# Sums of the resident operand made ahead and parked in DRAM, and result tiles added to the rows in DRAM by accumulating DMAs

## The reference, cut to what matters

```python
def reference(x, mem, ...):                     # x (1, 2048, 1024) fp32, D_FF = 4096
        h = _rmsnorm(x, norm_mix_g[layer])
        proj = h @ w_in[layer]
        ...                                     # window attention, pooling, memory attention
        merged = (gates[:, :, 0] * (y_attn @ w_branch_attn[layer])
                  + gates[:, :, 1] * (y_pool @ w_branch_pool[layer])
                  + gates[:, :, 2] * (y_mem @ w_branch_mem[layer]))
        x = x + merged @ w_out[layer]
        hm = _rmsnorm(x, norm_mlp_g[layer])
        x = x + jnp.square(jax.nn.relu(hm @ w_up[layer])) @ w_down[layer]
    return _rmsnorm(x, norm_final_g)
```

## Time and profile before

| what | value |
|---|---|
| median of 3 runs | 3003.94 us (2999.12 to 3004.13) |
| the profiled execution: time, span | 3000.8 us, 2999.1 us |
| busy: PE, DVE, ACT, POOL | 2736.9, 1779.3, 994.4, 968.1 us |
| granted TensorE clock over the span | 0.959 |
| first part (to 1317 us) | 1317 us |
| second part, first matmul to last | 1333.5 to 2983.4 us |

### The profile page before, as it was taken

One profiled execution on the slowest core, in us unless ns is written; L12 is line 12 of the kernel. 1 busy time (PEld: TensorE's weight loads), 2 busy tenths in 40 slices (PEclk: granted clock), 3 DMA queues, 4 the chain that ended last, 5 costly groups with the idle time before them and its releaser, 6 DMA issues.

```text
span 2999.1 us, 33978 instructions
## 1 busy us (share of the span) xinstructions
PE 2736.9 (91%) x12449; PEld 2245.0 (75%) x12449; DVE 1779.3 (59%) x2098; ACT 994.4 (33%) x1714; POOL 968.1 (32%) x621
## 2 busy tenths in 40 slices
PE   8999999999999999967878999799988969789697
PEld 7788778887888778856767888688877758667586
DVE  4643355244633363357677666866676686775987
ACT  4543244324433353333233222322232232321342
POOL 0101110020001010134453332333345666665765
PEclk9999999999999999988988999899999989989899
DMA  5124322332233323343553334333343534535343
GB/s 183 53 85 133 113 64 81 120 124 81 67 121 104 95 70 112 106 147 112 168 169 116 110 111 137 107 109 111 110 158 136 186 131 137 183 133 172 138 146 134
DMA packets 276351, 365.48 MB, mean 122 GB/s; under 512 B 10024, under 2 KB 219996, under 8 KB 276188
## 3 DMA queue, kind: packets, MB, share of 16 engines
q1 hardware_dynamic: 273884, 355.01, 36.3%
q0 software_dynamic: 2304, 8.39, 0.8%
HBM read 271.09 MB, written 92.27 MB: 121 GB/s over the span
## 4 chain that ended last, share of the span: by engine, by line
PE 62%; issue 13%; POOL 10%; DVE 9%; DMA 5%; ACT 1%; SPq 0%; POOLq 0%; DVEq 0%; ACTq 0%
PE ps L1404 19%; PE ps L1405 19%; PE ps L1406 19%; POOL rows_tm L1366 5%; PE ps L1409 2%; DMA piece_f<-mrg_d 2%; DMA piece_f<-up_d 2%; DVE s_lo L1098 2%; DVE res_lo L1107 1%; POOL s_sum L1342 1%; POOL s_sum L1337 1%; PE ps L1554 1%; DVE rows_tm L1184 1%; PE ps L1537 1%; POOL piece_f L1339 1%
## 5 line engine op out<-in xcount | busy, mean ns | idle before, releaser
L1404 PE MATMUL ps<-res_hi,s_hi 128*128 128x512 f32 x2016 | 810.7, 402 | 179.7 <-issue 121.4
L1405 PE MATMUL ps<-res_lo,s_hi 128*128 128x512 f32 x2016 | 802.0, 398 | 0.0
L1406 PE MATMUL ps<-res_hi,s_lo 128*128 128x512 f32 x2016 | 800.6, 397 | 0.0
L1404 PEld LDWEIGHTS ps<-res_hi,s_hi 128*128 128x128 f32 x2016 | 390.5, 194 | 278.1 <-issue 152.6
L876 DVE TENSOR_TENSOR w_lo<-stage,w_hi 128x2048 fp32r<-128x2048 f32 (+1 forms) x125 | 234.9, 1879 | 459.1 <-ACT w_hi L589 459.1
L1404 PE MATMUL ps<-h_hi,w_hi 128*128 128x512 f32 x1216 | 485.0, 399 | 11.6 <-issue 11.6
L1406 PE MATMUL ps<-h_hi,w_lo 128*128 128x512 f32 x1216 | 476.6, 392 | 0.0
L1405 PE MATMUL ps<-h_lo,w_hi 128*128 128x512 f32 x1216 | 476.3, 392 | 0.0
L1098 DVE TENSOR_TENSOR s_lo<-piece_f,s_hi 128x512 fp32r<-128x512 f32 x288 | 283.9, 986 | 289.8 <-ACT s_hi L589 289.8
L1406 PEld LDWEIGHTS ps<-res_hi,s_lo 128*128 128x128 f32 x2016 | 388.9, 193 | 83.1
L1405 PEld LDWEIGHTS ps<-res_lo,s_hi 128*128 128x128 f32 x2016 | 390.3, 194 | 80.2
(11 more groups left out here) (170 smaller groups left out, 3332.2 us busy)
## 6 DMA issues: line engine op xcount, KB each, us to landing
stage<-in_w_gate SPq DMA_DIRECT2D x96, 512.0 KB, 4.5
rows_d<-rows_tm SPq DMA_DIRECT2D x32, 1024.0 KB, 5.1
piece_f<-in_w_up SPq DMA_DIRECT2D x32, 1024.0 KB, 6.2
up_d<-c SPq DMA_DIRECT2D x128, 256.0 KB, 2.4
piece_f<-up_d SPq DMA_DIRECT2D x32, 1024.0 KB, 7.6
rows_tm<-rows_d SPq DMA_DIRECT2D x32, 1024.0 KB, 5.5
stage<-in_w_in SPq DMA_DIRECT2D x60, 512.0 KB, 4.7
src<-in_w_down SPq DMA_DIRECT2D x12, 1024.0 KB, 11.3
```

Source lines behind the costliest of these rows:

```text
L1404: mm(dst, wh, xh, start=first, stop=False)
L1405: mm(dst, wh, xl, start=False, stop=False)
L1406: return mm(dst, wl, xh, start=False, stop=last)
```

## The change

**Resident sums.** They are no longer made at the turns. For the jobs whose resident is a weight (0, 3, 4, 5, 6) GpSimd makes them in the first part, at the start of each of the 4 blocks: for each job it loads two 128 x 1024 tiles (512 KB each) into a new buffer `tin`, makes four sums of 128x512 in place and stores the two tiles to a DRAM tensor `t_d`; five times in a row, each after the last one's stores have landed. For jobs 1 and 2 it does the same inside units 5 and 6 (two tile pairs each) and 10, 12, 14 and 16 (one pair each), as `ht_d` gets ready (`up_load`, `up_sums`). At a turn SP now loads all seven operands ready made (`load_slot`): slots 0 and 1 into `src` some units ahead, slots 2 to 6 straight into `res_raw`, each once the last unit's product of the same number is done.

**Rows.** Only jobs 0 and 6 still have rows in SBUF, and there DVE does the additions (`add_row`). In jobs 3, 4 and 5 (24 units) GpSimd issues four DMAs of 256 KB per unit that add the tile to the rows in DRAM (`add_in_place`); the loads and stores of `rows_tm` in these jobs are gone. A tile may be written anew when its DMA of the unit before has landed (`c_free`).

**Further.** `piece_f` has two buffers and SP loads piece n + 2 in unit n. Relu and square go from one DVE instruction to two of ACT. ACT scales the rows to be transposed, each half with a signal of its own. The factor of the norm is folded into the gain. The moving sums are made in the order S1, S3, S2, S4, and the order of the splits at a turn is changed.

```diff
+JOBS = 7
+W_JOBS = [0, 3, 4, 5, 6]
+
+UP_SUMS = {5: (1, (0, 1)), 6: (1, (2, 3)), 10: (2, (0,)), 12: (2, (1,)), 14: (2, (2,)), 16: (2, (3,))}
...
-    return 0 <= n < N_OUT or FIRST[3] <= n < NQT
+    return 0 <= n < N_OUT or FIRST[6] <= n < NQT
+
+
+def adds_apart(n):
+
+    return FIRST[3] <= n < FIRST[6]
...
+                if s < 2:
+                    sp.dma_start(src[:, s], slot_of(j, s)).then_inc(src_ld[s], 16)
+                    return
+                if j:
+                    sp.wait_ge(prod, PROD * (FIRST[j] - 1) + s + 1)
+                sp.dma_start(res_raw[:, s], slot_of(j, s)).then_inc(raw_ld[s - 2], 16)
...
-                sp.dma_start(piece_f[:], piece_of(n)).then_inc(pc_ld, 16)
+                sp.dma_start(piece_f[:, n % 2], piece_of(n)).then_inc(pc_ld[n % 2], 16)
...
+                    load_piece(n + 2)
+                if n in (N_OUT - 1, FIRST[2] - 3) or starts(n + 3) and n + 3 >= FIRST[3]:
+
+                    sp.wait_ge(r_lo_done, PROD * (j + 1))
+                    if j < 2:
+                        sp.wait_ge(up_t_st[0], 64 if j == 0 else 192)
+                        sp.wait_ge(up_t_st[1], 64)
+                        for r in range(2):
+                            sp.wait_ge(ht_st[r], 16 * 4 * (j + 1))
+                    for s in range(2):
+                        load_slot(j + 1, s)
...
-                    load_b21(job_of(n + 1))
+                            sp.wait_ge(add_st[s], 16 * (n - FIRST[3]))
+                    load_rows(n + 1)
+                if last:
+                    load_slot(j + 1, 2)
+                store_up(n, 0, c22, 1, 1)
+                if last:
+                    load_slot(j + 1, 3)
+                    load_slot(j + 1, 4)
+                store_up(n, 1, c11, 0, 0)
...
+            def relu_sq(n, which, order):
+
+                if not squares(n):
+                    return
+                tile, done = c_tile(n, which), 4 * up_quartets(n) + order
+                act.wait_ge(ev_dve, 7 * n + which)
+                op(tile[:], tile[:], ACT.Relu).then_inc(relu, 1)
+                act.wait_ge(relu, done)
+                op(tile[:], tile[:], ACT.Square).then_inc(u_rdy, 1)
...
+            def norm_tiles(n):
+
+                if not 0 <= n < N_OUT:
+                    return
+                act.wait_ge(rs_pow, n + 1)
+                act.wait_ge(row_st[row_slot(n)], 16 * (slot_uses(n) + 1))
+                for i in range(2):
+                    t = rows_of(n)[:, i, :]
+                    op(t, t, ACT.Copy, scale=rrs[:, i:i + 1]).then_inc(xn_done, 1)
...
-            def t1(j):
-
-                for i in range(2):
-                    dve.wait_ge(src_ld[i], 16 * (j + 1))
-                if j:
-                    dve.wait_ge(prod, PROD * (FIRST[j] - 1) + S1 + 1)
-                v.tensor_tensor(res_raw[:, 2], src[:, 1], src[:, 0], ALU.subtract).then_inc(t_done, 1)
...
-            def t2(j):
-
-                dve.wait_ge(src_ld[2], 16 * (j + 1))
-                dve.wait_ge(r_lo_done, PROD * j + 1)
-                dve.wait_ge(t_done, 2 * j + 1)
-                v.tensor_tensor(src[:, 0], src[:, 2], res_raw[:, 2], ALU.subtract).then_inc(t_done, 1)
+                dve.wait_ge(r_hi_done, PROD * j + s + 1)
+                v.tensor_tensor(res_lo[:, s], r_src(s), res_hi[:, s].bitcast(F32), ALU.subtract).then_inc(r_lo_done, 1)
+
+            def c_free(n, s):
+
+                if N_OUT < n <= FIRST[3]:
+                    dve.wait_ge(up_st[s], 16 * up_quartets(n))
+                elif FIRST[3] < n <= FIRST[6]:
+                    dve.wait_ge(add_st[s], 16 * (n - FIRST[3]))
...
+            def add_row(n, which, i, cols):
+
+                if not adds_rows(n):
                     return
-                tile = c_tile(n, which)
                 dve.wait_ge(ev_dve, 7 * n + which)
-                v.scalar_tensor_tensor(out=tile[:], in0=tile[:], scalar=0.0, in1=tile[:], op0=ALU.max, op1=ALU.mult)\
-                    .then_inc(u_rdy, 1)
+                dve.wait_ge(row_in[row_slot(n)], 16 * (slot_uses(n) + 1))
+                dst = rows_of(n)[:, i, cols * TB:(cols + 1) * TB]
+                v.tensor_tensor(dst, dst, c_tile(n, which)[:], ALU.add).then_inc(row_add, 1)
...
             for n in range(NQT):
-                j, first, last = job_of(n), starts(n), starts(n + 1) and n + 1 < NQT
+                j, first, last = job_of(n), starts(n), turns(n)
                 if first:
                     r_low(j, 3)
                 s_low(n, 6)
                 take_u2(n)
                 if last:
                     r_low(j + 1, 0)
-                    t1(j + 1)
-                if n == FIRST[6] - 1:
+                if n == FIRST[6] - 2:
                     dve.wait_ge(gf_ld, 16)
                     v.tensor_scalar(g_fin[:], g_fin[:], float(D) ** 0.5, None, ALU.mult).then_inc(gf_rdy, 1)
...
+                if first:
+                    r_low(j, 4)
                 s_low(n + 1, 0)
-                if has_norm(n - 1):
-                    scale_tile(n - 1)
+                if first:
+                    r_low(j, 5)
+                if last:
+                    r_low(j + 1, 1)
+                if is_final(n - 1):
+                    final_tiles(n - 1)
+                take_c22(n)
                 if first:
                     r_low(j, 6)
-                    r_low(j, 4)
-                    r_low(j, 5)
...
+                if last:
+                    r_low(j + 1, 2)
+                take(n, C21, A22, u3, 2)
+                add_row(n, C21, 1, 0)
...
+            def resident_sums(t, done, loaded):
+
+                b11, b12, b21, b22 = t[:, 0, 0:TB], t[:, 0, TB:D], t[:, 1, 0:TB], t[:, 1, TB:D]
+                pool.wait_ge(*loaded)
+                g_.tensor_tensor(b11, b12, b11, ALU.subtract).then_inc(t_sum, 1)
+                g_.tensor_tensor(b12, b22, b12, ALU.subtract).then_inc(t_sum, 1)
+                pool.wait_ge(t_sum, done * 4 + 1)
+                g_.tensor_tensor(b22, b22, b11, ALU.subtract).then_inc(t_sum, 1)
+                pool.wait_ge(t_sum, done * 4 + 3)
+                g_.tensor_tensor(b21, b21, b22, ALU.subtract).then_inc(t_sum, 1)
...
+                k1 = pool.snap(b + 4)
+                for i, j in enumerate(W_JOBS):
+                    k0 = 0 if j == 0 else KT * (j - 3)
+                    whole = w_outv if j == 0 else w_downv
+                    done = b * len(W_JOBS) + i
+                    if i:
+                        pool.wait_ge(t_st, done * 32)
+                        g_.tensor_tensor(flag[:, 3 + i:4 + i], m_half[:, 0:1], m_half[:, 0:1], ALU.add)
+                    for half, kb in enumerate((b, k1)):
+                        pool.dma_start(tin[:, 0, half, :], whole[:, bass.ds(kb + k0, 1), :].rearrange("p k n -> p (k n)"))\
+                            .then_inc(t_ld, 16)
+                    resident_sums(tin[:, 0], done, (t_ld, done * 32 + 32))
+                    pool.wait_ge(t_sum, done * 4 + 4)
+                    g_.tensor_tensor(flag[:, 8 + i:9 + i], m_half[:, 0:1], m_half[:, 0:1], ALU.add)
+                    for half, kb in enumerate((b, k1)):
+                        pool.dma_start(t_v[j][:, bass.ds(kb, 1), :].rearrange("p k n -> p (k n)"), tin[:, 0, half, :])\
+                            .then_inc(t_st, 16)
...
+            def up_load(j, ks):
+
+                if ks[0]:
+                    for i in range(len(ks)):
+                        pool.wait_ge(up_t_st[i], 32 * (uses(j, ks[i]) - 1))
+                for r in range(2):
+                    pool.wait_ge(ht_st[r], 16 * 4 * j)
+                pool.wait_ge(r_lo_done, PROD * j)
+                for i, k in enumerate(ks):
+                    for half in range(2):
+                        pool.dma_start(tin2[:, i, half, :], whole_of(j)[:, 4 * half + k, :]).then_inc(up_ld[i], 16)
+
+            def up_sums(j, ks):
+
+                for i, k in enumerate(ks):
+                    resident_sums(tin2[:, i], unit(j, k), (up_ld[i], 32 * uses(j, k)))
+                    pool.wait_ge(t_sum, 4 * unit(j, k) + 4)
+                    for half in range(2):
+                        pool.dma_start(t_v[j][:, 4 * half + k, :], tin2[:, i, half, :]).then_inc(up_t_st[i], 16)
+
+            def add_in_place(n, which, s, i, cols):
+
+                if not adds_apart(n):
+                    return
+                if n == FIRST[3]:
+
+                    for r in range(2):
+                        pool.wait_ge(row_st[r], 16 * (N_OUT // 2))
+                pool.wait_ge(ev_dve, 7 * n + which)
+                q = (n - FIRST[3]) % N_DOWN
+                pool.dma_start(rows_v[q][:, i, cols * TB:(cols + 1) * TB], c_tile(n, which)[:], accum_op=ALU.add)\
+                    .then_inc(add_st[s], 16)
...
             for n in range(NQT):
-                j, first, last = job_of(n), starts(n), starts(n + 1) and n + 1 < NQT
-                add_tile(n - 1, C12, 0, 1)
-                if first:
-                    t4(j)
+                if n in UP_SUMS:
```

(19 more changed lines are left out.)

301 lines of the change are left out of this document (129 added, 172 removed).

## The result

The changed kernel takes 2811.18 us (median of 4 runs, 2809.92 to 2819.84), the kernel before on the same chip 3002.78: a ratio of 0.937, 95% interval 0.9349 to 0.9391. The profiled execution of the changed kernel took 2819.84 us (span 2818.2), that of before 3000.8. It is the longest of the four, 8.7 us above the median, so what the two profiles show is 181 us of the 192 that the medians give.

The account below looks back on a forecast made before the run. It took TensorE's 19.04 us a unit as the floor, and the chain of sums, split and low part as the bound at turns. Terms -16 - 16 - 6 - 32 - 81 - 24 - 4 + 5 = -174 took 3000.8 to 2826 us, range 2785 to 2890.

Parts of the forecast that it names:

- Start of the second part: First part: GpSimd's added rounds of loads, sums and stores slow DVE now and then; +5 us, between 0 and 25.
- Rival (2): First part: GpSimd's rounds take 22 us, window sums come late and TensorE waits; +45 us, 2871 us; chance 0.08.
- Unit 0: Start of the second part: with slots loaded ready made, unit 0 takes 32 us for 47.9; -16 us.
- Units 1 to 5: Job 0: the wait for the scaled rows before the transposes goes, the ht wait stays; -16 us.
- Units 6 to 8: Job 1's sums, late slots and the norm's order still cost time: 28 + 35 + 30 = 93 for 99.2; -6 us.
- Turns 24 and 40: Up stores delay the slots, leaving small stalls: 27.5 us a turn for 44.0 and 43.0; -32 us.
- Turns 48, 56 and 64: No stores between the slots: 22.5 us for 49.5 and 50.3, 23.5 for 49.4 in unit 64; -81 us.
- Late units: Jobs 3 to 5 and 6: the piece no longer waits behind the rows' store and one buffer; -24 and -4 us.
- Accumulating DMAs: Jobs 3 to 5: each tile takes 5 us to landing, with 14 us available; cost 0 us.
- (1): Turns stay half long: slots land late in other DMA traffic, five turns at +10 us; 2876 us; chance 0.18.
- (3): Jobs 3 to 5: accumulating DMAs pass one after another and bound the units; 3138 us at 8 us each; chance 0.07.
- (4): Better than counted: job 0 at its floor and no contention; 2795 us; chance 0.05.

Follow-up runs that it names:

- the norm first: Changed kernel, but in unit 7 ACT squares and scales the rows before splitting slots 0 and 1, and VectorE's low parts come later; 2807.0 us.
- orders only: Changed kernel with GpSimd's moving sums ahead of its store waits and loads in units 5 and 6, slots 0 and 1 issued first in unit 7; 2799.9 us.
- staged loads: Orders only, plus each GpSimd load waits for its own buffer, the power stands between the loads, and unit 6's rows are stored before the slots; 2796.2 us.
- the order carried through: Staged loads, plus S4 ahead of job 1's sums, unit 7's power first, unit 6's rows scaled earlier, low parts behind the ht takes; 2789.9 us.

## Why the prediction was right, and where its steps were not

The time (2826 against 2811) and the range held. By its terms, in the two profiled executions (3000.8 to 2819.8, -181 for -174; by the medians it is -192):

- **Start of the second part, +5:** +2.5 (first matmul at 1336.0 for 1333.5); over the eleven experiments on the changed kernel, whose first part is the same, it came between 1327.1 and 1337.0, and the mean of the twelve kernels is 1330.6, 3 us below before. Rival (2) is out. That the term is above zero is not shown.
- **Unit 0, -16:** -18.6 (29.3 us). Right, a little small.
- **Units 1 to 5, -16:** -5.2. The term was -13.6 in units 1 to 4, as expected, and +8.4 in unit 5. Of the 13.6, 11.8 hang on the second buffer (105.4 us with one for 93.6), and not on ACT's scaling alone. The step that failed: the prediction put GpSimd's sums for job 1 "in units 5 and 6", but charged them to unit 6 alone. In unit 5 too GpSimd waits for a store (14.5 us idle), and what stands behind is not only the power but S2, ACT's split of it, and so the norm; and its sums hold up VectorE, so that the second transposes wait 5.78 us (1.14 without the sums). The prediction's own sign, 10 us or less of idle time before the transposes in units 1 to 5, did not come: it is 16.9 us for the 22.3 of the earlier trace rows.

```profile
L1492 PE MATMUL ps<-ident,rows_tm 128*128 128x128 f32 x80 | 12.7, 310 | 16.9 <-DVE ht L1236 12.6 <-ACT rows_tm L641 4.3
```

- **Units 6 to 8, -6:** -3.7 (30.7 + 35.3 + 29.5; the prediction had 28 + 35 + 30). Right in size: the four profiles with this order give 93.4 to 96.9 us for the three, though unit 7 alone varies from 35.3 to 43.3. Its reason for unit 7, ACT's split of slot 0 ahead of the squares, was one of three waits in a row: with it gone (the norm first), VectorE's low part took its place, and after that (orders only, staged loads) the rows' store and S4. With the order carried through it takes 28.1.
- **Turns 24 and 40, -32:** -40.7 (23.2 and 23.1 for the 27.5 predicted). The landings were right: slot 6 is there 12.3 us into unit 24, 12 was counted. The stalls behind were sized too large, 6.8 us in all for 4.1 (in unit 24 products 2, 3 and 5 take 3.75, 4.20 and 4.12 us for 2.72), and the contention of 1.7 us that it added isn't there.
- **Turns 48, 56 and 64, -81:** -83.4. Right to 1.2 us a turn. But the attribution was wrong. "A turn is the chain sums, split, low part" was read at the turn into unit 24 and carried to all; at the turn into 48 ACT waited 8.60 us for the piece first. The sums removed from the kernel before are worth 36.6 us over the five turns, and the second buffer, for which the prediction had no term there, 72.7 us (184.8 against 112.1). The number came out since the sum was made from the changed kernel's own times, in which the piece was early.
- **Late units, -24 and -4:** -24.3 and -4.0. Right. The prediction had "both go"; by the runs with rows in SBUF and with one buffer, either the second buffer (with the additions on VectorE) or the accumulating DMAs would have done in jobs 3 to 5. Job 6 has no such DMAs and needs the buffer: units 65 to 71 take 155.4 us with one for 133.4. In units 65 to 71 VectorE is 115.7 us busy of 133.4, 16.5 a unit, above the 15 predicted and below 19.04; before it was 110.8 of 137.5.
- **Accumulating DMAs, 0 us:** the 5 us assumed for a tile are 5.4. Right, and between turns twice as many cost nothing.
- **The rivals:** (1) is out, no turn is near 32 us and the clock stays at 1.00; (2) and (3) are out, see above; (4), job 0 at its floor, fell for units 5 to 8.
- **After the last matmul, no term:** -3.3 (12.4 us for 15.7). The last additions are made by VectorE between the gatherings and no longer by GpSimd behind them; that this is the reason is not shown.

The prediction's sentence on VectorE's two-input operations weighed them for job 6, where nothing came of it; the place where they bit, GpSimd's four sums in a row in unit 5, was not looked at. The sum was right partly by luck: units 1 to 5 came out 10.8 us above their term and the turns 24 and 40 8.7 us below theirs. Two sums are off by one: the five turns are 141 us over the floor, not 142, and 3000.8 - 174 is 2826.8.

## What to carry to other kernels

Read each kind of turn by itself in the trace before naming its bound: two that take as long may wait for different things. When a buffer is doubled together with other edits, cost the other edits without it; here they give 42 to 45 us alone and the buffer decides about the rest. And before moving a wait or a DMA issue on one engine, walk the in-order queues of all engines behind it up to the one that sets the time, since moving only the nearest operation (the power here) gives nothing.

## What the runs showed of the hardware

- A VectorE operation on 128x512 with two SBUF inputs takes 0.69 us alone, and 3.9 to 4.9 us when it meets three of GpSimd's additions (1.27 us each) issued without a gap. There are 28 that long in the changed kernel and the eleven experiments on it, and none in the two without GpSimd's sums for job 1. All 28 ended 0.55 us after the third addition, also the nine that are recorded as begun 0.1 to 0.5 us ahead of the first. Shorter hold-ups end the same way: of the changed kernel's 567 such operations from unit 0 on, all 159 that took over 0.8 us ended 0.55 us after one of GpSimd's. A gap of 0.08 us, where GpSimd's fourth sum waits for a semaphore, let VectorE in, and that sum then took 1.62 us. VectorE's gatherings, with one input in PSUM, took 0.67 to 0.69 us throughout. The Trainium skill (SBUF — State Buffer, SBUF: two separate sides) says that whichever starts first holds the shared port pair for its whole instruction and the other is blocked. The trace agrees that it is a block and no shared rate; but the wait ran over three instructions, not one, and fell on VectorE even where its record begins first.
- Accumulating DMAs of 256 KB from SBUF to DRAM: 5.4 us to landing with four in 19 us, 8.8 and 10.1 us with eight, the plain store 2.5. GpSimd spends 0.87 us on issuing one.
